# Block two's gates: high weights against both halves of the activations in one 512-column matmul

## What is computed

```python
u = rms_norm_2(h, norm_mix[i])
q, k, v, c, g = jnp.split(u @ w_in[i], splits, axis=-1)
...
g_attn, g_conv = jnp.split(jax.nn.sigmoid(g), 2, axis=-1)
h = h + (g_attn * y_attn + g_conv * y_conv) @ w_o[i]
```

## Time and profile before

| | |
|---|---|
| median of 3 runs | 2121.27 us (2120.89 to 2122.17) |
| profiled execution | 2120.77 us |
| its span, first to last instruction | 2118.8 us |
| mean granted TensorE clock | 1.000 |
| TensorE, weight loads, VectorE, ScalarE busy | 99%, 90%, 77%, 58% |
| HBM traffic over the span | 199 GB/s |

### The profile page before, as it was taken

The page is one execution under the profiler, slowest core; times in us unless marked ns, Lnnn a source line. Parts: engine busy times, 40 slices in busy tenths (PEclk is TensorE's granted clock), DMA queues, the critical chain, the costliest instruction groups (busy, mean ns, idle before and its releaser), DMA issues.

```text
span 2118.8 us, 39051 instructions
## 1 busy us (share of the span) xinstructions
PE 2096.6 (99%) x16284; PEld 1904.1 (90%) x16284; DVE 1638.4 (77%) x2519; ACT 1237.1 (58%) x2010; POOL 13.1 (1%) x20
## 2 busy tenths in 40 slices
PE   8999999999999999999999999999999999999999
PEld 6898999999998999998888989888898888998888
DVE  7899789888887788877886656887688764788876
ACT  4765656555755655555655547665575644666554
POOL 0000000000000000000000000000000000000000
PEclk9999999999999999999999999999999999999999
DMA  9566467767644467655555654555555557445553
GB/s 367 202 218 211 178 214 254 245 232 279 227 160 171 159 216 236 206 180 189 185 192 188 229 161 150 200 190 192 187 181 191 190 192 220 140 170 209 189 189 129
DMA packets 122098, 424.55 MB, mean 200 GB/s; under 512 B 13457, under 2 KB 22033, under 8 KB 121154
## 3 DMA queue, kind: packets, MB, share of 16 engines
q1 hardware_dynamic: 121922, 422.06, 57.6%
HBM read 417.68 MB, written 4.33 MB: 199 GB/s over the span
## 4 chain that ended last, share of the span: by engine, by line
PE 90%; DVE 4%; ACT 4%; DMA 1%; issue 1%; POOL 0%; SPq 0%; ACTq 0%; DVEq 0%
PE bank L207 89%; ACT arena L259 2%; DVE arena L214 1%; DVE lo L214 1%; ACT hi L259 1%; DMA raw<-W 1%; PE bank L211 1%; DVE arena L222 1%; ACT L259 0%; DVE ada L231 0%; DMA xT<-x 0%; DVE m L214 0%; ACT L251 0%; ACT ych L259 0%; POOL arena L214 0%
## 5 line engine op out<-in xcount | busy, mean ns | idle before, releaser
L207 PE MATMUL bank<-h,hi 128*128 128x256 f32 (+1 forms) x5248 | 1183.2, 312 | 0.0
L259 ACT ACTIVATE hi<-raw 128x1024 fp32r<-128x1024 f32 x656 | 689.1, 1057 | 542.1 <-PE bank L207 474.5
L207 PE MATMUL bank<-h,lo 128*128 128x256 f32 x3328 | 949.7, 285 | 0.1
L207 PEld LDWEIGHTS bank<-h,hi 128*128 128x128 f32 x5248 | 861.4, 190 | 61.0 <-issue 2.6
L214 DVE TENSOR_TENSOR lo<-raw,hi 128x1024 fp32r<-128x1024 f32 x656 | 791.8, 1219 | 93.7 <-ACT hi L259 92.7
L207 PEld LDWEIGHTS bank<-h,lo 128*128 128x128 f32 x3328 | 633.7, 190 | 12.2 <-issue 8.1
L207 PE MATMUL bank<-act,hi 128*128 128x512 f32 x1056 | 370.0, 393 | 0.0
L207 PE MATMUL bank<-act,lo 128*128 128x256 f32 x1056 | 294.7, 279 | 0.0
L207 PEld LDWEIGHTS bank<-act,hi 128*128 128x128 f32 x1056 | 197.9, 187 | 47.1
L207 PEld LDWEIGHTS bank<-act,lo 128*128 128x128 f32 x1056 | 197.9, 187 | 0.0
L259 ACT ACTIVATE arena<-arena 128x256 f32<-128x256 f32 (+4 forms) x202 | 98.4, 493 | 158.6 <-DVE arena L214 151.0
(11 more groups left out here) (152 smaller groups left out, 1946.1 us busy)
## 6 DMA issues: line engine op xcount, KB each, us to landing
raw<-W SPq DMA_DIRECT2D x664, 512.0 KB, 3.3
ada<-WA SPq DMA_DIRECT2D x80, 512.0 KB, 3.8
arena<-WA SPq DMA_DIRECT2D x16, 512.0 KB, 14.1
arena<-conv_rows SPq DMA_DIRECT2D x16, 280.0 KB, 5.8
arena<-taps SPq DMA_DIRECT2D x2, 1792.0 KB, 9.0
p_projected<-arena SPq DMA_DIRECT2D x2, 1024.0 KB, 7.8
arena<-scr SPq DMA_DIRECT2D x16, 128.0 KB, 5.2
arena<-p_projected SPq DMA_DIRECT2D x2, 1024.0 KB, 4.8
```

The costliest lines, as they stand in the source:

```text
L207: return self.done(lambda e: e.matmul(out, l, r, start=start, stop=stop, skip_group_check=True))
L259: return self.done(lambda e: e.activation(out, in_, f, scale=scale, **kw))
```

## The change

The gates of block two are made with `wide` instead of `pair`, with `MAIN` as the pool: one bank for each column block of 128 features, so two uses for each item instead of one. For each column block ScalarE copies the second sum from PSUM to `dst`, VectorE adds the first sum from PSUM to it, which frees the bank, and the product with `var_t` is then made on `dst` in SBUF. ScalarE now counts its tiles in two steps of 8, with the copy of a column block behind each.

```diff
--- before.py
+++ after.py
@@ -712,14 +712,14 @@
                             if ends:
                                 f.tick()
 
-            def wide(name, l, x, outs, turns, nk=KD, ready=None):
+            def wide(name, l, x, outs, turns, nk=KD, ready=None, pool=WIDE):
 
 
                 banks = {}
                 for k, n in turns:
                     use, m = outs[n]
                     if k == 0:
-                        banks[n] = take(WIDE, use)
+                        banks[n] = take(pool, use)
                     wh, wl, ends = tile([(name, l, k, ("c", m))])
                     ready(k)
                     pe.mm(t256(banks[n], 0), wl, t256(x, 2 * k), k == 0, False)
@@ -1269,7 +1269,8 @@
                     f.chain(("att2", q[0]), att2_steps(q[0]), attention2(q[0]))
                 elif what == "gate2":
                     l, p = q
-                    pair(MAIN, item, "w_in_2", l, [("c", 1792 + (2 * p + j) * 128) for j in range(2)], h_in(("mx", l)))
+                    wide("w_in_2", l, hw, [((*item, j), 1792 + (2 * p + j) * 128) for j in range(2)],
+                         [(k, n) for n in range(2) for k in range(KD)], ready=lambda k: pe.wait_ge(v_main, ("h", ("mx", l), k)), pool=MAIN)
                 elif what == "attn out":
                     l, p = q
                     pair(MAIN, item, "w_attn_out_2", l, [("c", (2 * p + j) * 128) for j in range(2)],
@@ -2005,8 +2006,12 @@
                     l, p = q
                     f.tiles(16)
                     dst = (gA if p < 4 else gC)[:, (p % 4) * 512:(p % 4 + 1) * 512]
-                    v.wait_ge(pe_main, item)
-                    v.tt(two(dst), two(ps(item)), bc(var_t, 1, [128, 2, 256]), MUL).then_inc(v_main, item, frees=item)
+                    for j in range(2):
+                        use = (*item, j)
+                        v.wait_ge(a_main, ("share", *use))
+                        v.tt(t256(dst, j), t256(ps(use), 0), t256(dst, j), ADD).then_inc(v_main, ("sum", *use), frees=use)
+                    v.wait_ge(v_main, ("sum", *item, 1))
+                    v.tt(two(dst), two(dst), bc(var_t, 1, [128, 2, 256]), MUL).then_inc(v_main, item)
                 elif what == "attn out":
                     l, p = q
                     f.tiles(8)
@@ -2594,7 +2599,13 @@
                 elif what == "gate2" or what == "gate2 last":
                     l = q[0]
                     if what == "gate2":
-                        f.tiles(16)
+                        p = q[1]
+                        dst = (gA if p < 4 else gC)[:, (p % 4) * 512:(p % 4 + 1) * 512]
+                        for j in range(2):
+                            use = (*item, j)
+                            f.tiles(8)
+                            a.wait_ge(pe_main, use)
+                            a.act(t256(dst, j), t256(ps(use), 1), ACT.Copy).then_inc(a_main, ("share", *use))
                     p = 7 if what == "gate2 last" else q[1] - 1
                     if p >= 0:
                         dst = (gA if p < 4 else gC)[:, (p % 4) * 512:(p % 4 + 1) * 512]
```

## The result

The changed kernel takes 2129.86 us (median of 6 runs, 2128.50 to 2130.82), the kernel before 2120.93 (6 runs beside it, 2120.69 to 2122.17): 1.0042 of it, 95% interval 1.0032 to 1.0051. It is slower by 8.9 us. (Of all the executions in this document one, of the kernel with both mends, took 4335.05 us; it is left out of that kernel's median.) The profiled executions took 2129.21 and 2120.77 us, spans 2127.3 and 2118.8.

The account below looks back on a forecast made before the run. TensorE, busy 99% of the span, was taken as the bound; per layer +3.0 us in the gates and +1.4 behind them, +8.8 for both, gave 2129.6 and a median of 2130 us; range 2122 to 2137, likeliest 2126.5 to 2133.

Parts of the forecast that it names:

- shorter matmuls: Gates: one 512-wide matmul replaces two of 256 columns, 0.0136 us less per weight tile, -1.74 us a layer.
- wait at half 5, behind the scores: Gates, halves being 8 tiles: TensorE waits 2.1 us for the bank VectorE's half-2 addition frees after the scores.
- wait at half 10, copy behind the exponential: Gates: ScalarE's copy of half 7 stands behind the second exponential, so TensorE waits 0.7 us for that bank.
- wait at half 15, behind the output of attention: Gates: half 12's bank comes free only after VectorE handles the second attention output; TensorE waits 1.8 us.
- wait at half 9: Gates: a further small TensorE wait of about 0.1 us a layer.
- copy, addition, product, split behind the variance: Behind the gates: this work delays the normalisation 2.5 us, of which 1.4 us a layer was taken to reach silu.
- a clock that falls in the waits: Sign of being wrong: the granted clock falling while TensorE waits; no size given.
- silu 1.0 or 1.75 later: Behind the gates: 1.0 us if the table load is done before ScalarE waits for the normalisation, 1.75 if after.
- as busy time alone: Gates: 5.1 us on ScalarE and 6.0 on VectorE a layer fit their idle time, so costed at nothing.
- A: Rival, gates: banks come free in time, only the 3.5 us gain is seen, 2117.8 us; chance 0.08.
- B: Rival, gates: only the odd half behind the scores waits, +1.8 us a layer, 2124.8 us; chance 0.14.
- C: Rival, gates: lateness feeds itself, halves 7, 11 and 13 wait too, +6 to +7.5 a layer, 2134 to 2136 us; chance 0.18.

Follow-up runs that it names:

- both mends: Changed kernel with four banks for the gates and the mended last pair, no other edit: 2122.07 us, ratio 1.0005.
- mended last pair: Changed kernel with, in the last pair only, ScalarE's copy of half 15 and VectorE's pair-7 work moved ahead of the last side step: 2128.77 us, ratio 1.0040.
- work-alone run: Kernel before, one bank a pair and 256-column matmuls, with as many copies and additions and the product from SBUF: 2128.64 us, ratio 1.0036.
- four banks: Changed kernel with four banks in turn for the gates from pair 2 on, conv mean and variance in the attention's banks: 2123.51 us, ratio 1.0012.
- the first experiment: Changed kernel with each half's copy and addition ahead of the split and side step behind it, product ahead of the last: 2132.72 us, ratio 1.0055.
- banks alone: Kernel before with one half-filled bank for each column block and the product in two of 256 columns, no copies or additions: 2127.68 us, ratio 1.0032.

## Why the prediction was right

The mechanism was right: three waits for VectorE's additions at the halves named, and a later stretch behind the gates. That the median came out within 0.2 us of the forecast is in part luck (below). The forecast was 2130.0 us, +8.8 on the profiled execution; measured were 2129.86 and +8.44. Its terms for a layer, and what layer 0 of the first profile has:

| step | forecast | measured |
|---|---|---|
| shorter matmuls | -1.74 | -1.4 |
| wait at half 5, behind the scores | 2.1 | 2.2 |
| wait at half 10, copy behind the exponential | 0.7 | 0.7 |
| wait at half 15, behind the output of attention | 1.8 | 1.5 |
| wait at half 9 | 0.1 | none |
| ahead of scores 0, no wait recorded | none | 0.14 |
| sum of the gates | 3.0 | 3.14 |
| copy, addition, product, split behind the variance | 1.4 | 1.07 |
| the layer | 4.4 | 4.21 |

**Shorter matmuls.** The two mends together have a single wait of 1.9 us in the gates (out 0) and reach the variance 0.53 later than before, so the wide form gave 1.4. The pace of a tile inside a run was right; in the six runs of halves between two side steps 0.02 to 0.15 us each are lost, why was not looked for. This gain was put 0.35 too large.

**Luck.** That term makes the layer dearer than forecast; the wait at half 15, the one at half 9 and the stretch behind the gates came out cheaper, by 0.3, 0.1 and 0.33, so the errors largely cancel. The forecast also put the median 0.5 above the profiled execution, as the three runs before had it. In the six runs of the kernel before beside the result it is 0.16; in the changed kernel it is 0.65, and three of its six executions have the lower mean clock that goes with a fall (last section). The forecast had no such falls: a clock that falls in the waits stood among its signs of being wrong, and that sign came, in two of three profiles, at some 1.5 us each. It changes the size of the cost and not its places.

**The bank order.** Shown: without the work it costs 3.44 a layer; with one bank more the three waits are gone. The addition behind the scores was placed to 0.3 us (1261.7 against 1261.97).

**Behind the gates.** Of my two cases, silu 1.0 or 1.75 later, the first held: the table load at 1313.62 came before the normalisation had ended at 1314.26. The mended last pair takes 0.87 of the 1.07 back.

**What the prediction did not have.** It charged the added work only where it held up a bank or the stretch behind the variance, and "as busy time alone" nothing. But in the kernel before TensorE comes to out 0 only 0.8 us after the last of the attention's copies on ScalarE:

```profile
1279.05 2.02 ACT L259 ACTIVATE arena<-bank 128x512 f32<-128x512 f32 x4
...
1281.85 1.95 PE L207 MATMUL bank<-arena 128*64 128x256 f32 x16
```

More than 0.8 us of added work ahead of those copies therefore holds TensorE up. How much it costs in all depends on where it stands. The work-alone run shows 3.54 a layer, but it has both copies behind the pair and loses 1.68 behind the variance, where the changed kernel loses 1.07. With the work placed as in the change, four banks lose 1.60 a layer although the matmuls gain 1.37, so there the work costs 2.97: 1.9 at out 0 and 1.07 behind the variance. In the changed kernel the wait at out 0 does not show, since TensorE arrives late as well. The two costs, 3.44 for the banks and 2.97 for the work, thus lie partly over each other: they give 4.2 + 1.4 = 5.6 and not 6.4. Taking the bank waits away gave back 2.6 and not 3.44.

**The rivals.** A (the banks come free in time) is out by the three waits. B (only the first wait) is out by the other two. C (more halves wait) did not come: halves 7, 11 and 13 do not wait in any profile of the changed kernel.

## What to carry to other kernels

A pool's depth is a time: banks times the work per bank. Halving what a bank holds halves it, and the test is not whether the consuming engine has idle time but when, in its in-order queue, it reaches the evacuation: put a trace row's end against the time at which the producer asks again. Work that is added to engines with idle time is free only off the chain of small steps between them; when two causes hold the same engine up, measure each alone, since mending one shows only what the other does not cover. The prize here was 1.4 us a layer, and no version was shown to beat the kernel before.

## What the hardware showed beside it

The granted clock fell behind single waits of TensorE. Over nine profiles with the wide form in all pairs (three of the changed kernel and the six variants of it) there are 18 waits of 1.88 to 1.91 us as the timeline counts them. Behind 5 of them the clock went to the lower level, 1.2 GHz (windows of 4 us at 0.57 to 0.66), each time for 3 to 4 us, which cost about 1.5 us; behind the other 13, at the same places in the same code, it stayed at 1.00. Behind the two waits of 3.05 and 3.15 us in the first experiment it fell both times, the second time for some 7 us at a cost of 2.8; behind the ones of 1.7 us and less (banks alone, work alone) never. Why it falls behind one wait and not behind the next is open. The Trainium skill (TensorE: Matmul & The Clock Gate, Loop structure matters more than you think) warns of long waits between every two matmuls; here one wait in a stream without gaps was enough, but not always. This is also most of the spread of the changed kernel's six runs, 2.3 us: the three with a mean granted clock of 1.000 took 2128.50 to 2129.32 us, the three with 0.999 took 2130.41 to 2130.82.
